# Second block's modulation product taken off TensorE: GpSimd multiplies by silu(c) rows, ScalarE sums, in ring slots between the dense ones

## Time and profile before

| | |
|---|---|
| median of 3 runs | 1752.6 us (1751.82 to 1757.37) |
| span of the profiled execution | 1752.9 us |
| TensorE busy | 1691.3 us, 96% |
| VectorE busy | 920.8 us, 53% |
| ScalarE busy | 698.2 us, 40% |
| GpSimd busy | 41.9 us, 2% |
| granted TensorE clock, mean | 0.991 |
| loads | 401.39 MB read, 230 GB/s over the span |

### The profile page before, as it was taken

The page is one execution under the profiler, slowest core; times in us unless marked ns, Lnnn a source line. Parts: engine busy times, 40 slices in busy tenths (PEclk is TensorE's granted clock), DMA queues, the critical chain, the costliest instruction groups (busy, mean ns, idle before and its releaser), DMA issues.

```text
span 1752.9 us, 28605 instructions
## 1 busy us (share of the span) xinstructions
PE 1691.3 (96%) x11122; PEld 1325.4 (76%) x11122; DVE 920.8 (53%) x1620; ACT 698.2 (40%) x1261; POOL 41.9 (2%) x32
## 2 busy tenths in 40 slices
PE   7999999999989999999999999999999999999997
PEld 5778999987779999977889999897545454545453
DVE  4976666439767665466856588765221212121212
ACT  2255444321365443364653477733223232322222
POOL 0000000000000000004120000000000000000000
PEclk9999999999999999999999999998999999999999
DMA  7544444545434555532422343446699999999993
GB/s 287 195 161 169 151 180 178 184 148 220 172 142 173 188 191 192 186 115 82 138 72 97 121 140 125 140 162 264 272 418 421 422 422 422 422 422 422 422 422 159
DMA packets 63956, 404.04 MB, mean 231 GB/s; under 512 B 13056, under 2 KB 14592, under 8 KB 15232
## 3 DMA queue, kind: packets, MB, share of 16 engines
q1 hardware_dynamic: 63440, 401.34, 59.1%
q10 hardware_dynamic: 432, 1.51, 0.2%
HBM read 401.39 MB, written 1.44 MB: 230 GB/s over the span
## 4 chain that ended last, share of the span: by engine, by line
PE 85%; DVE 10%; ACT 4%; issue 1%; DMA 0%; SPq 0%; DVEq 0%; ACTq 0%
PE ps L861 24%; PE ps L1460 20%; PE ps L1007 10%; PE ps L668 6%; PE ps L1433 4%; PE ps L1450 4%; DVE big L2269 2%; DVE inv L2504 2%; PE ps L1340 1%; DVE wlo L2682 1%; PE ps L1372 1%; PE ps L690 1%; PE ps L1401 1%; ACT wb L1885 1%; PE ps L1351 1%
## 5 line engine op out<-in xcount | busy, mean ns | idle before, releaser
L2332 DVE TENSOR_TENSOR wlo<-ring,whi 128x2048 fp32r<-128x2048 f32 x76 | 174.2, 2292 | 113.2 <-ACT whi L1659 112.9
L861 PE MATMUL ps<-hg_hi,wlo 128*128 128x272 f32 (+1 forms) x672 | 191.4, 285 | 0.0
L861 PE MATMUL ps<-hg_hi,whi 128*128 128x272 f32 (+1 forms) x672 | 191.0, 284 | 0.0
L861 PE MATMUL ps<-hn_lo,whi 128*128 128x272 f32 (+1 forms) x672 | 190.8, 284 | 0.0
L1460 PE MATMUL ps<-big 128*64 128x512 f32 x816 | 181.8, 594 | 0.7 <-ACT big L2165 0.7
L1460 PE MATMUL ps<-ring,big 128*64 128x512 f32 x816 | 181.7, 594 | 0.0
L1659 ACT ACTIVATE whi<-ring 128x2048 fp32r<-128x2048 f32 x76 | 144.9, 1907 | 75.8 <-PE ps L861 75.1
L668 PE MATMUL ps<-hn,ring 128*128 128x272 f32 x640 | 156.2, 400 | 9.3 <-DVE hn L2240 5.9
L668 PEld LDWEIGHTS ps<-hn,ring 128*128 128x128 f32 x640 | 120.3, 192 | 40.1 <-issue 16.9
L1460 PEld LDWEIGHTS ps<-big 128*64 128x64 f32 x816 | 57.4, 137 | 107.0 <-issue 106.6
L1460 PEld LDWEIGHTS ps<-ring,big 128*64 128x64 f32 x816 | 57.1, 137 | 107.2 <-issue 106.8
(11 more groups left out here) (453 smaller groups left out, 3538.8 us busy)
## 6 DMA issues: line engine op xcount, KB each, us to landing
ring<-in_stream SPq DMA_DIRECT2D x277, 1024.0 KB, 5.0
big<-in_stream SPq DMA_DIRECT2D x102, 1024.0 KB, 12.5
h<-in_xT SPq DMA_DIRECT2D x1, 1088.0 KB, 5.0
out_xT<-h SPq DMA_DIRECT2D x1, 1024.0 KB, 4.7
big<-in_consts ACTq DMA_DIRECT2D x1, 896.0 KB, 4.9
cst<-in_consts SPq DMA_DIRECT2D x1, 576.0 KB, 6.0
big<-in_consts ACTq DMA_DIRECT2D x1, 326.5 KB, 3.3
from_blocks<-big SPq DMA_DIRECT2D x1, 256.0 KB, 2.0
```

What stands on the lines that cost most here:

```text
L861: m = mm(out, a[:, at_:at_ + P], b[:, kept], start=first and i == 0, stop=last and i == 2)
L2332: v.tensor_tensor(wlo[j][:, :], ring[:, j, :], whi[d % 3][:, :], ALU.subtract).then_inc(wlo_ready, 1)
```

## The change

- `w_ada_2` is laid out with outputs on partitions: one slot holds 2 x 128 outputs, each with its 1024 inputs in a row. The 12 ada slots of a layer leave the `w_in` slots and stand between the dense ones, in the order of `BEHIND_IN` ("o" is `w_out`, "g" `w_gate_up`, "d" `w_down`, "a" ada).
- silu(c) becomes a tile `cs` of 128 x 1024 with c in each partition, loaded behind the first six ring slots. ScalarE takes its silu in layer 0 behind the four silus of the convolution's output.
- GpSimd multiplies each ada slot in place by `cs` (128x2048, one instruction). ScalarE then sums each half of 1024 with a Copy that has `accum_out`, straight into a column of `mod` (`ada_sums`), two dense slots later in its order (`after_weights`).
- TensorE's `mod_rows` and `mod_columns` are gone, as are ScalarE's `rows_out` and `columns_out`, the buffer `row_sb`, and their PSUM turns in `WORK`.
- The ring slot of an ada slot is free when ScalarE has summed it (`ada_done`); `slot_done` now counts TensorE's 48 slots of a layer, and all waits on it are shifted. The loops over `w_gate_up` on TensorE, ScalarE and VectorE and SyncE's first loop are unrolled.

```diff
-IN_ORDER = ("glu0 ada0 glu1 ada1 glu2 ada2 glu3 ada3 qk0 ada4 v01 ada5 qk1 ada6 qk2 ada7 qk3 ada8 v23 ada9 ada10 ada11").split()
+IN_ORDER = "glu0 glu1 glu2 glu3 qk0 v01 qk1 qk2 qk3 v23".split()
+BEHIND_IN = "o o a o o g a" + 9 * " g g a" + 3 * " g" + 3 * " d" + " a" + 9 * " d"
+DENSE_POS, ADA_POS = ([IN_SLOTS + i for i, kind in enumerate(BEHIND_IN.split()) if (kind == "a") == ada] for ada in (False, True))
...
-            sp.dma_start(small[:, 40:48], par2_d[:, QC:QC + DC]).then_inc(loaded, 16)
             for j in range(RING):
                 sp.dma_start(ring[:, j, :], stream[j, :, :]).then_inc(ring_full[j], 16)
+            sp.dma_start(cs[:, :], args["c_rows"]).then_inc(ada_loaded, 16)
             def refill(i, j):
-                sp.wait_ge(slot_done, i - RING + 1)
+                if isinstance(i, int) and i - RING < B2:
+                    l, at_ = divmod(i - RING, LAYER_SLOTS)
+                    if at_ in ADA_POS:
+                        sp.wait_ge(ada_done, l * ADA_SLOTS + ADA_POS.index(at_) + 1)
+                    else:
+                        before = at_ if at_ < IN_SLOTS else IN_SLOTS + DENSE_POS.index(at_)
+                        sp.wait_ge(slot_done, l * PE_SLOTS + before + 1)
+                else:
+                    sp.wait_ge(slot_done, i - RING + 1 - BY_ADA)
...
-                def mod_rows(u):
-                    w = weights(IN_ORDER.index(f"ada{u}"))
-                    bank = take(f"a{u}")
-                    for k in range(DC):
-                        r = slice(32 * (k % 4), 32 * (k % 4) + 32)
-                        m = mm(bank[r, 0:2 * P].rearrange("p (n c) -> p n c", n=2), cs[:, k, :], w[:, k, :, :],
-                               start=k < 4, stop=k >= 4, tile_position=(0, 32 * (k % 4)))
-                    m.then_inc(slot_done, 1)
-                def mod_columns(p):
-                    bank = take(f"m{p}")
-                    W(pe, "row_out", 2 * p + 2, l)
-                    for u in range(2):
-                        for n in range(2):
-                            c = 2 * u + n
-                            m = mm(bank[:, c:c + 1], row_sb[:, u, n * P:(n + 1) * P], ones[:, 0:1], start=True, stop=True)
-                    m.then_inc(mod_cols, 1)
...
+                def ada_sums(u):
+                    W(act, "ada_times", u + 1, l)
+                    for n in range(2):
+                        o = ADA_SLOTS * 2 * l + 2 * u + n
+                        w = ring[:, ADA_POS[u] % RING, n * D:(n + 1) * D]
+                        m = f(w, w, ACT.Copy, accum_out=mod[:, o:o + 1])
+                    m.then_inc(ada_done, 1)
+                def after_weights(d):
+                    for u, at_ in enumerate(ADA_POS):
+                        if DENSE_POS[d - 1] < at_ + 2 <= DENSE_POS[d]:
+                            ada_sums(u)
...
+                if l == 0:
+                    act.wait_ge(ada_loaded, 16)
+                    f(cs[:, :], cs[:, :], ACT.Silu).then_inc(cs_ready, 1)
...
+                def gate_on_act(i):
+                    W(act, "gate_scaled", 2 * i + 1, l)
                     f(sgu[:, i % 2, kept], sgu[:, i % 2, kept], ACT.Silu).then_inc(gate_act, 1)
+                    high_weights(OUT_SLOTS + 3 + i)
+                    W(act, "hff_ready", i + 1, l)
+                    f(hff_hi[:, i, kept], hff[:, i, kept], ACT.Copy).then_inc(hff_hi_ready, 1)
+                    after_weights(OUT_SLOTS + 3 + i)
...
+                if l == 0:
+                    pool.wait_ge(cs_ready, 1)
+                c_row = cs[:, :].rearrange("p (a b) -> p a b", a=1).to_broadcast([P, 2, D])
+                for s in ADA_POS:
+                    pool.wait_ge(ring_full[s % RING], (l * (LAYER_SLOTS // RING) + s // RING + 1) * 16)
+                    w = ring[:, s % RING, :].rearrange("p (a b) -> p a b", a=2)
+                    nc.gpsimd.tensor_tensor(w, w, c_row, ALU.mult).then_inc(ada_times, 1)
```

More of the change, by code:

```diff
@@ L536, in inverses_back @@
                         sp.dma_start(to[r, :, r], from_blocks[r, i].rearrange("q r c -> r q c")).then_inc(small_moved, 16)
[L538 to L542, removed]
+            T1 = (B2 + ORDER.index("V0")) // RING + 3
+            for i in range(RING, T1 * RING):
                 refill(i, i % RING)
@@ L790, in _ @@
                 scores(0)
-                mod_rows(5)
                 chunk("qk1", 0, "q1")
@@ L794, in _ @@
                 scores(1)
-                mod_columns(2)
                 chunk("qk1", 1, "k1")
@@ L812, in _ @@
                 weigh(1)
-                mod_rows(7)
                 chunk("qk3", 0, "q3")
@@ L828, in _ @@
                 weigh(2)
-                mod_rows(8)
                 chunk("v23", 0, "V2")
@@ L882, in _ @@
                 add_out(0, conv_part, True, False, [0])
-                mod_rows(11)
                 weigh(7)
                 turn_probs(8)
-                mod_columns(5)
                 weigh(8)
@@ L926, in _ @@
                 first_gate_up()
-                for i in range(1, 4):
+                for i in range(1, GU_SLOTS):
                     gate_up(i, need=i - 1 if i >= 2 else None)
-                with pe.Fori(0, (GU_SLOTS - 4) // RING) as t:
-                    for i in range(RING):
-                        gate_up(4 + i, t0=t, need=t * RING + i + 3)
                 d0 = OUT_SLOTS + GU_SLOTS
@@ L1584, in chunk_out @@
                     else:
-                        W(act, "even_full", [name for name in IN_ORDER if name[:3] != "ada"].index(slot_name) + 1, l)
+                        W(act, "even_full", IN_ORDER.index(slot_name) + 1, l)
                 def work(name, n):
@@ L3047, in first_block_stream @@
         for name in IN_ORDER:
-            if name in pairs:
-                parts += chunk_pairs(w, [pairs[name]])
-            else:
-                i = 24 * l + 2 * int(name[3:])
-                parts += chunk_pairs(x["w_ada_2"][0], [(i, i + 1)])
-        parts += chunk_pairs(x["w_out"][l], [(2 * i, 2 * i + 1) for i in range(4)])
-        parts += chunk_pairs(x["w_gate_up"][l], [(i, FC + i) for i in range(FC)])
+            parts += chunk_pairs(w, [pairs[name]])
+        dense = chunk_pairs(x["w_out"][l], [(2 * i, 2 * i + 1) for i in range(4)])
+        dense += chunk_pairs(x["w_gate_up"][l], [(i, FC + i) for i in range(FC)])
         v = x["w_down"][l].reshape(FC, P, DC, P)
@@ L3058, in first_block_stream @@
                 part = v[4 * g:4 * g + 4, :, 4 * half:4 * half + 4, :].transpose(1, 0, 2, 3).reshape(P, -1)
-                parts.append(np.concatenate([part, np.zeros((P, SLOT - part.shape[1]), np.float32)], 1)[None])
+                dense.append(np.concatenate([part, np.zeros((P, SLOT - part.shape[1]), np.float32)], 1)[None])
+        rows = x["w_ada_2"][0][:, 3 * D * l:3 * D * (l + 1)].T.reshape(ADA_SLOTS, 2, P, D).transpose(0, 2, 1, 3).reshape(ADA_SLOTS, 1, P, SLOT)
+        taken = {"ada": iter(rows), "dense": iter(dense)}
+        parts += [next(taken["ada" if kind == "a" else "dense"]) for kind in BEHIND_IN.split()]
     return parts
```

150 lines of the change are left out of this document (50 added, 100 removed).

## The result

The changed kernel takes 1820.13 us (median of 4 runs, 1817.95 to 1825.83) where the kernel before takes 1753.38 on the same chip (4 runs). The ratio is 1.037, with an interval of 1.0352 to 1.0388: slower, as forecast, but by 67 us instead of 24, and above the range of 1750 to 1812. The span of the profiled execution went from 1752.9 to 1818.6 us, 65.7 more.

What follows compares the result with a forecast made beforehand. TensorE, busy 96% of 1752.9 us, was taken as the bound. Terms: -5.6 and -2.5 (layers 0, 1), -0.2 (start), +2.0 (clock), +12.6 (out), +18.0 (gates) = +24.3, giving 1777 us; range 1750 to 1812.

Steps and rivals of the forecast that it cites:

- closed loop of 13.1 us: Gate stage: product, gate product, copy, sums, refill and semaphores take 13.1 us per pair, 1.0 over TensorE's.
- Removal: Projections: TensorE's removed modulation work gains 7.0 us per layer, 5.6 in layer 0, of at most 33.4 in all.
- The clock: TensorE's longer waits can leave it at the lower clock: 1 us per layer charged, between 0 and 3.
- The product's length: GpSimd: 4.5 us for a 128x2048 product, 12 products per layer.
- Layer 1's convolution: A product falls into VectorE's gapless stretch: 4.5 us lost, bounds 0 and 4.5; layer 1 gains 2.5.
- Out stage: Both layers: products of slots 16 and 19 delay VectorE; 6.3 us of TensorE waiting per layer, bounds 0 and 8.4.
- Gate stage: Both layers: eight products cost 1.0 us each and 1 at entry, 9 us per layer; bounds 0 and 21.
- Down stage, ring, start: Down stage's one product 0; ring 0, at worst 0.5 us per ada slot; start gains 0.2.
- locks badly: Rival: gate stage costs 21 to 25 us instead of 9, total 1801 to 1809; chance 0.18.
- Only convolution and out stage pay: Rival: gate-stage lateness stays under 4 us; 1759, or 1753 with half the out stage's price; chance 0.16.
- the products hide: Rival: held VectorE operations find slack everywhere, or the hold isn't for a whole long instruction; 1742; chance 0.14.
- TensorE was last everywhere: Rival: all 33.4 us of removed TensorE work come back, 1719; chance 0.02.

Runs made afterwards that it cites:

- The fillers: Unread matmuls, 3 and 10 ahead of the first scores, added to the changed kernel with each product in 8 instructions: 1759.46 us, ratio 1.0013.
- Experiment 2: Changed kernel, but ScalarE sums one column instead of 1024: 1819.79 us (one run).
- experiment 3: Changed kernel with `hff_lo` of a gate slot issued behind the next slot's two scalings: 1785.92 us, ratio 1.017.
- experiment 4: Changed kernel with each GpSimd product in 8 instructions of 128x256 instead of one of 128x2048: 1762.38 us, ratio 1.0029.
- placed behind: Changed kernel with each product in 8 instructions and no modulation slot before the fifth gate slot: 1749.45 us, ratio 0.9963.
- experiment 7: Changed kernel, but GpSimd fills the slot with zeros instead of multiplying; only the second block's start is read, 723.39 us.

## Why the prediction was wrong

The mechanism was right, and its size in one stage was not. The failed step is in the gate stage, as the prediction put it: the product "can overlap the scalings or the wait for the high part", and of a closed loop of 13.1 us and VectorE's 13.2 to 14.2 us "I take this lower one, since ScalarE's high part runs meanwhile". Point by point:

- **Removal.** TensorE was last in the dense part and not in the projections; 7.0 us per layer were forecast of 33.4 in all. Without products the first block ended 9.1 us earlier, where the forecast's terms without products give 11.1 (1752.9 less 1742). The order is right.
- **The clock.** I charged 1 us per layer. The fillers gave back 1.7 to 2.1 us in layer 0: the low clock ate most of the gain up to mu (0.2 us left of 2.5). The forecast's bound of 3 held it; I had the wait of 5.5 us before my eyes ("up to 5.7 us, for k0") and took half of what it cost.
- **The product's length.** 4.5 us forecast, 4.81 measured on average; part of it is GpSimd waiting for VectorE, since the first two take 4.51 and 4.60.
- **Layer 1's convolution.** Forecast: one tap of 5 us. Fourteen taps took 11.00 us at 479.51 and 6.73 before; the longest tap is 4.76 us. So 4.3 us for the 4.5.
- **Out stage.** Forecast 6.3 per layer, measured 7.9 and 8.2. Slot 19's product came as put down: `low_weights` of 168.32 took 6.65 us. The first one held another instruction than the `low_weights` that I had named (its row is below); TensorE's sums then waited 4.83 us at 178.23 and ran at the lower clock (2.18 us for 4).
- **Gate stage.** Forecast 9 per layer, measured 22.4 and 26.2, over the upper bound of 21. Three things were wrong in it. I counted by capacity: VectorE has 1.3 and 0.65 us of waiting per slot, so part of a product fits in. But the waiting lies in front of `low_weights` and of the scalings, and seven of the eight products got their turn at `hff_lo` (the first met `low_weights`, 6.32 us at 197.00, with no TensorE wait behind it). A held instruction keeps those behind it from starting, though their operands are ready. So nothing overlapped: 2 x 5.3 + 4.4 = 15.0 us. Seven such pairs, each less TensorE's 12.1, are 20.4 us, and 2.0 came at the entry, where TensorE ran at a granted clock of 0.50 (179.8 to 184.2 us): together the 22.4. In layer 1, with 256 tokens, TensorE's pair would be 11.3 us and the pair took 14.9, which is 25 of the 26.2. Second, I took the loop over sums and refill as the pace, which was the shorter of the two candidates; of two loops that both must close, the longer one sets the pace. Third, that loop was counted per pair. A freed ring slot serves the slot six places on, which is the second next modulation slot, so its 13.1 us stand against two pairs of TensorE's, 24.2. In the trace it closes over 30.1 us (238.33 to 268.46), 18.2 of them between the end of the product and ScalarE's turn to sum it. Experiment 2 shows that the sums loop is not it, experiment 3 that the order on VectorE is (34 us), experiment 4 that the whole-instruction hold is (58 us).
- **Down stage, ring, start.** The down slot's product does not run in w_down: it begins at 328.46 us and holds one more `hff_lo` (4.84 us at 329.44), with no wait of TensorE behind it. For the ring and the start no wait shows; 0 is not contradicted.
- **The second block.** 3.8 us more in the profiled pair, without a part of the change there. Across the kernels above the stretch from there to the end varies by 4 us (1024 to 1028 us in those that compute the same), and in the kernel after the granted clock is 0.92 from 862 to 952 us, where the kernel before has 0.97 in about the same part (800 to 887). I can't tie it to the change, and leave it open.

Of the rivals, "locks badly" came nearest, at 1801 to 1809, with 21 to 25 us per gate stage. It had the product right before the gate product, with ScalarE's next silu behind it; the lock was on the low part instead. "Only convolution and out stage pay" (1753 to 1759) is near what the cut products gave in their old places, 1762 us, and "the products hide" (1742) near what they gave placed behind, 1749. "TensorE was last everywhere" was not seen in any run.

The Trainium skill (SBUF — State Buffer, "SBUF: two separate sides") says that whichever of the two starts first has the shared port pair for the whole instruction, and it names two kinds of VectorE instructions: those with two SBUF inputs, and those in a 2-port mode. The trace agrees for the first: 4.85 us for `hff_lo` beside a product of 4.94. The second may be this one-input instruction of the out stage, beside the product of 158.52 (4.60 us), where it takes 0.36 otherwise; in which mode it ran no trace shows:
```profile
159.01 4.26 DVE L2389 TENSOR_SCALAR big<-h,par 128x272 f32<-128x272 f32 x1
```
It also says that two SBUF inputs clash only with a GpSimd instruction that reads SBUF; experiment 7 agrees, for a fill of 1.81 us that lay whole among the two-input taps of the convolution, while the one-input instruction was held by a fill as well.

## What to carry to other kernels

When GpSimd work is put beside VectorE work, don't compare busy shares. Take the longest GpSimd instruction, ask which VectorE instruction stands next when it starts, and what stands in order behind that one; add the whole instruction to that chain for every time they meet. If it can't be avoided, cut the GpSimd work into instructions as short as VectorE's own (58 of 67 us here, for the same products), and place it where another engine sets the pace (another 12 by the ratios). An engine that is freed of work begins to wait, and can come out of the waits at half the clock: fill the wait, but by the measured length of the filler.

## What the runs showed that I had not expected

- A one-input `TENSOR_SCALAR` with its output in SBUF was held (4.26 us instead of 0.36), and a 128x1 `TENSOR_TENSOR` as well (2.01 us instead of 0.16). The addition to h in front of it, with one operand in PSUM, began beside the same product at 158.54 and took its usual 0.43.
- Eight pieces of 128x256 take 1.08 us each on average, 8.1 us in all beside VectorE in the stretch shown (5.8 to 10.3 elsewhere in layer 0), for what one instruction does in 4.8, and the kernel gains 58 us by it.
- GpSimd writes 128x2048 in 1.82 us where the product of that size takes 4.8. Such a fill held no instruction with two operands in SBUF, and it did hold a `TENSOR_SCALAR` with one (1.53 us instead of 0.36).
- Where a product begins is set by the engine that it holds: in the gate stage each but the first came at the same point of VectorE's order, a pair later.
- Twenty fillers of one `mm` each are forty matmul records of 0.24 us: 9.33 us.
